# ScalarE's one-hots spread over two tiles, an earlier gate load, and doubled row slots moved to other tiles

## The reference, cut to what matters

```
g   = softmax(best_s)                                  # 8 heads x 16 experts
act = gelu(einsum('thkd,td->thk', u_tab[expert], x)) * g
out = einsum('thk,thkd->td', act, v_tab[expert])
```

## Time and profile before

| | us |
|---|---|
| three runs, median | 2750.67 |
| lowest and highest | 2739.39, 2750.81 |
| the profiled execution | 2743.88 |
| its span, first to last instruction | 2742.1 |
| tiles 26 to 89 of scoring | 1221.82 to 1678.12 |
| tiles 106 to 121 | 1797.25 to 1898.80 |
| the seam: last two tiles of scoring to the first of combining | 1920.66 to 1955.10 |
| combining | 1955.10 to 2718 |

### The profile page before, as it was taken

The page is one execution under the profiler, slowest core; times in us unless marked ns, Lnnn a source line. Parts: engine busy times, 40 slices in busy tenths (PEclk is TensorE's granted clock), DMA queues, the critical chain, the costliest instruction groups (busy, mean ns, idle before and its releaser), DMA issues.

```text
span 2742.1 us, 34124 instructions
## 1 busy us (share of the span) xinstructions
PE 2401.4 (88%) x10438; PEld 1873.8 (68%) x10438; DVE 2054.3 (75%) x3817; ACT 1140.9 (42%) x2430; POOL 982.4 (36%) x665
## 2 busy tenths in 40 slices
PE   4987888999899787888888889999688999999996
PEld 3767766666456566666776767778567777777775
DVE  4867713666388855888887888866678888888888
ACT  2332043444311143236666667786233333333333
POOL 2013104422032321684675856686212222222220
PEclk9999999999999899999999999999899999999998
DMA  7646654333032325577989989899899999999996
GB/s 275 218 162 253 255 218 154 123 123 113 25 119 101 146 77 188 129 180 263 313 248 311 283 274 298 272 301 357 319 377 368 369 388 388 392 390 389 393 389 237
DMA packets 276170, 697.78 MB, mean 254 GB/s; under 512 B 52832, under 2 KB 164832, under 8 KB 234848
## 3 DMA queue, kind: packets, MB, share of 16 engines
q1 hardware_dynamic: 182624, 384.03, 39.8%
q0 software_dynamic: 74496, 270.70, 28.5%
q10 hardware_dynamic: 18944, 41.95, 4.2%
HBM read 614.67 MB, written 81.92 MB: 254 GB/s over the span
## 4 chain that ended last, share of the span: by engine, by line
PE 48%; DVE 21%; ACT 8%; DMA 7%; DVEq 5%; issue 5%; ACTq 4%; SPq 1%; POOL 0%; PEldq 0%; PEld 0%
PE ps L897 26%; PE ps L588 7%; PE ps L573 4%; DVE arena L1492 3%; ACTq L1350 3%; DMA act_in<-act_scratch 2%; DVEq L1856 2%; PE ps L937 2%; PE ps L600 2%; DVE g_acc L1844 2%; DVE rows L1835 2%; DVE t_lo L1915 2%; DMA arena<-in_weights 2%; ACT hot L1302 1%; DMA ring<-in_weights 1%
## 5 line engine op out<-in xcount | busy, mean ns | idle before, releaser
L1282 ACT CAST t_hi<-raw 128x1024 fp32r<-128x1024 f32 x256 | 268.6, 1049 | 726.5 <-PE ps L897 707.8
L2045 POOL DMA_INDIRECT rows<-in_rows,pick_e x256 | 289.2, 1129 | 779.7 <-DVE g_acc L1844 719.3
L2056 POOL DMA_INDIRECT gate_scratch<-cell_g,cell x256 | 454.1, 1774 | 157.5 <-DVE cell_g L1830 81.6
L897 PE MATMUL ps<-t_hi,c_hi 128*128 128x512 f32 x1024 | 408.5, 399 | 65.5 <-DVE t_lo L1915 45.9
L897 PE MATMUL ps<-n_hi,t_hi 128*128 128x512 f32 x1024 | 413.1, 403 | 31.9 <-DVE t_lo L1861 23.1
L1980 POOL TENSOR_TENSOR w_lo<-ring,w_hi 128x1024 fp32r<-128x1024 f32 x76 | 190.5, 2512 | 666.4 <-ACT w_hi L1035 559.1
L897 PE MATMUL ps<-n_lo,t_hi 128*128 128x512 f32 x1024 | 404.2, 395 | 0.0
L897 PE MATMUL ps<-n_hi,t_lo 128*128 128x512 f32 x1024 | 403.6, 394 | 0.0
L897 PE MATMUL ps<-t_hi,c_lo 128*128 128x512 f32 x1024 | 400.9, 391 | 0.0
L897 PE MATMUL ps<-t_lo,c_hi 128*128 128x512 f32 x1024 | 400.8, 391 | 0.0
L1844 DVE SCALAR_TENSOR_TENSOR g_acc<-rows,small,g_acc 128x1024 f32<-128x1024 f32 x254 | 326.4, 1285 | 94.0 <-ACT small L1351 78.2
(11 more groups left out here) (207 smaller groups left out, 3939.5 us busy)
## 6 DMA issues: line engine op xcount, KB each, us to landing
raw<-in_table SPq DMA_DIRECT2D x256, 512.0 KB, 8.5
ring<-in_weights SPq DMA_DIRECT2D x44, 2048.0 KB, 8.2
act_scratch<-act_out SPq DMA_DIRECT2D x128, 256.0 KB, 4.3
act_in<-act_scratch SPq DMA_DIRECT2D x128, 256.0 KB, 10.7
gate_in<-gate_scratch SPq DMA_DIRECT2D x32, 1024.0 KB, 13.8
arena<-in_weights ACTq DMA_DIRECT2D x24, 1024.0 KB, 9.4
gate_scratch<-score_in SPq DMA_DIRECT2D x16, 1024.0 KB, 11.9
gate_scratch<-staged ACTq DMA_DIRECT2D x8, 2048.0 KB, 9.6
```

The lines of the kernel that those rows point to most:

```text
L897: last = mm(out, a, b_, start=start and x == 0, stop=stop and x == len(pairs) - 1, skip_group_check=True)
L1282: copy(t_hi[:, t % 2, :], raw[:, t % 4, :]).then_inc(hi_ready, 1)
L2045: G.indirect_dma_start(rows[:, j % 4, :], None, rows_in, bass.IndirectOffsetOnAxis(ap=pick_e[:, j:j + 1], axis=0)).then_inc(row_in[j % 4], 16)
L2056: G.indirect_dma_start(gate_cells, bass.IndirectOffsetOnAxis(ap=cell[:, n:n + 1], axis=0), cell_g[:, n:n + 1], None, compute_op=ALU.add).t ...
```

## The change

`scale_hot` is cut in two. The Abs part becomes `spread_hot`; for steps 1 to 31 it is issued at the end of the tile before the step's own, and for step 0 and steps 32 to 63 where it was. The Relu part stays. The wait for the step two before moves with the Abs. `slots_of` gives the tiles 124 to 127 one slot each, the even tiles 106 to 120 two, and in combining every eighth tile two (16 of them) where it was every sixth (20). On SP the first gate load, with the waits ahead of it, moves from behind the last two stores of activations to behind the raw load of tile 131, one tile earlier in the program. The buffers of `t_hi` and `t_lo` stay at two.

```diff
--- before.py
+++ after.py
@@ -317,14 +317,12 @@
 
             if k < DENSE:
                 return ()
-            if k < P - 4:
-                return (k - DENSE,)
             if k < P:
-                j = P - 4 - DENSE + 2 * (k - P + 4)
-                return (j, j + 1)
+                j = k - DENSE + min(max(k - 105, 0) // 2, 8)
+                return (j, j + 1) if k % 2 == 0 and 106 <= k <= 120 else (j,)
             v = k - P
-            j = P - DENSE + 4 + v + min((v + 2) // 6, 20)
-            return (j, j + 1) if v % 6 == 3 and v < 120 else (j,)
+            j = P - DENSE + 8 + v + (v + 4) // 8
+            return (j, j + 1) if v % 8 == 3 else (j,)
 
         def starts(s):
             return 2 * s if s < DENSE // 2 else DENSE + 4 * (s - DENSE // 2)
@@ -499,16 +497,17 @@
                 for x in range(2, 2 * len(PAIRS)):
                     if starts(x - 1) == k:
                         load_scores(sp, False, x)
+                if k == P - 1:
+                    for half in range(2):
+                        sp.wait_ge(gates_stored[half], 16 * STEPS // 16)
+                        sp.wait_ge(scattered[half], 16 * TOPK * HEADS)
+                    load_gates(0, 0)
                 if k == P // 2:
                     for t in range(4):
                         load_act(0, t)
                 if k:
                     store_act(k - 1)
             store_act(P - 1)
-            for half in range(2):
-                sp.wait_ge(gates_stored[half], 16 * STEPS // 16)
-                sp.wait_ge(scattered[half], 16 * TOPK * HEADS)
-            load_gates(0, 0)
 
             def step(i, t, half, last=False):
 
@@ -1292,7 +1291,7 @@
                 act.wait_ge(tile_done, k + (P - 1))
                 copy(c_hi[:, t % 2, :], act_in[:, t % 4, :]).then_inc(c_hi_ready, 1)
 
-            def scale_hot(s):
+            def spread_hot(s):
 
                 col = 4 * (s % 32)
                 after(act, g_done, s - 1)
@@ -1300,6 +1299,10 @@
                     if s < 32:
                         A(hot1[:, s % 2, x, :], iota, ACT.Abs, bias=sel_n[:, 0, col + x:col + x + 1])
                     A(hot2[:, s % 2, x, :], iota, ACT.Abs, bias=sel_n[:, 1, col + x:col + x + 1])
+
+            def scale_hot(s):
+
+                col = 4 * (s % 32)
                 act.drain()
                 if s < 32:
                     A(hot1[:, s % 2], hot1[:, s % 2], ACT.Relu, bias=ones[:, 0:1], scale=-1.0)
@@ -1368,9 +1371,14 @@
                 if k - 1 in TURN_AT:
                     take_block(1 + TURN_AT.index(k - 1))
                 for s in steps_of(k):
+                    if s % 32 == 0 or s > 32:
+                        spread_hot(s)
                     scale_hot(s)
                     if s:
                         copy_gates(s - 1)
+                for s in steps_of(k + 1):
+                    if 0 < s < 32:
+                        spread_hot(s)
                 if k == P - 6:
                     copy_gates(STEPS - 1)
                 for j in slots_of(k)[1:]:
```

## The result

The changed kernel takes 2727.99 us, the median of ten runs (2720.88 to 2733.64), against 2750.74 for the kernel before in ten runs beside them: a ratio of 0.993, 95% interval 0.9914 to 0.9947. It is faster, by 22.8 us, about half of what I forecast.

A forecast was written before the change was run, and what follows sets the result against it. TensorE was busy 88% of the span, so time could come only from its waits, which differ by stage. Terms -31 + 9 - 15.5 - 7 = -44.5 took 2743.9 to 2699.4, forecast as 2700 us, 80% range 2678 to 2730.

The forecast's parts named there:

- Spreading: Score tiles, steps 1 to 31: moving the Abs a tile ahead removes waits for hot2g; -31 us, between -50.5 and -20.
- POOL's lag: Score tiles while a pair's scatters are sent: POOL falls behind 5.8 us a pair, 2 lost four times, 8 us.
- the 16 tiles over 108 us: Sign against the prediction: 16 score tiles, 112.8 us before and forecast near 103, staying over 108.
- The 39 us for VectorE alone: Score tiles: VectorE's 48.7 us of idle time less 9.6 that stays, the spreading gain before POOL's lag.
- Doubled slots: Tiles 106 to 120: eight added gathers on a full POOL cost +9 us, between 0 and +15.
- today's lead: Tiles 106 to 120: 4 us of the gathers' existing lead, counted once, taken off the cost of doubled slots.
- longer instructions: Tiles 106 to 120: 2 us added to the cost of doubled slots for longer scatters.
- bound of +15: Tiles 106 to 120: upper end of the forecast cost of the doubled slots, in us.
- POOL paces the trains and the doubled tiles: Rival for score tiles: POOL sets the pace, spreading gives only -20, doubled slots cost +15; 2716 us, chance 0.17.
- the rival that I held at 4 in 100: Scatters in the trains and doubled tiles stretch beside denser VectorE row work, making the kernel slower; 2771 us, chance 0.04.
- Seam: Between scoring and combining: gate load issued at 1923.6 instead of 1939.11, PE idle about 8 us; -15.5 us, -10 to -21.
- Combining: Combining half: 16 doubled tiles for 20 save 6.3 us, plus 0.7 at the first output block; -7 us, -5 to -9.

The follow-up runs named there:

- e7: Changed kernel with two scatters a tile from 24 to 95, no doubled tiles in scoring, all 24 in combining at every fifth tile; 2702.9 us, ratio 0.9853.
- e8: Changed kernel with two scatters a tile from 24 to the end of scoring, three in every eighth tile from 96; 2710.81 us, ratio 0.9878.
- e10: e7 with its 24 doubled combining tiles at every fourth tile instead of every fifth; 2711.86 us, ratio 0.9845.
- e9: Changed kernel with the sixteen doubled tiles of combining moved two tiles away from the gate load; 2730.5 us, ratio 0.9934.
- e1: Kernel before with only the Abs of steps 1 to 31 moved a tile ahead, old slots and gate load; 2731.1 us, ratio 0.9943.
- e3: Kernel before with only the first gate load moved ahead of the last two stores; 2741.1 us, ratio 0.9978.
- e4: Changed kernel with the slots of the kernel before, so spreading and early gate load only; 2721.6 us, ratio 0.9919.
- e5: The even pace: changed kernel with two scatters a tile from 24 to 95 in place of three and two; 2715.75 us, ratio 0.9884.

## Why the prediction was half right

*Spreading* (forecast -31, measured -19.5). The step itself was right: the Abs hide in the odd tile, and while rows are in time hot2g is too, in all but the tile of a pair's Exp. The step that failed is POOL's lag, 8 us. I had POOL's need for four tiles right, 27.1 us (27.2 measured, with shorter scatters and longer gathers than I took), but set it against 25.3 us for the tiles, a mean over 16 with the slow tile of the pair in it. While the scatters are sent, four tiles take 23.6 us, so POOL falls behind by 3.6 us and not by 1.8: 11.5 us in a pair's 12.8 tiles, not 5.8. The even pace gives 456.3 - 424.2 = 32 us (35.5 in e7, e8 and e10), and the bunched scatters take 12.6 to 16 of these where I had 8. I had said that the 16 tiles over 108 us would make the prediction wrong: they took 110.4.

The 39 us for VectorE alone were too many as well. That 16 tiles with an even pace take 103.4 us, where I had put them near 103, is partly luck: PE, which idles in only 3 of them, sets the pace in the rest, and the tile of a pair's Exp, of whose 4.4 us I let 2.5 go, kept 4.6.

*Doubled slots* (forecast +9, bound +15, measured +22.8): the largest miss. The eight gathers at 10.7 were not too few: six of them fall in the stretch. The two other parts were wrong. I took off 4 us for today's lead. It gave nothing lasting: POOL was full, and the row loop added 9.1 us of waiting instead. And I put 2 us for longer instructions, where 10.7 were lost. The bound of +15 held no room for either; a cost over 20 us was the second thing that I had named as proof of an error. My rival "POOL paces the trains and the doubled tiles" (2716) named the mechanism, at too low a price.

In the changed kernel 29 of the 38 scatters of that stretch overlap a row dot or row add and take 1.99 us on the mean, the nine others 1.60; before it was 25 at 1.82 and 14 at 1.57 (counted over the timelines of POOL and VectorE). So more of them met VectorE's row work, and those that did were longer. That is the mechanism of the rival that I held at 4 in 100, in one of its two places; in tiles 34 to 49 the scatters did not stretch (1.74 us for 1.83), only the gathers did (1.38 for 1.10). The overlap is a correlation in the traces; no run took VectorE's row work away from the scatters. The rule of the Trainium skill, "SBUF — State Buffer", Who interferes with whom, is that a VectorE instruction with two SBUF inputs contends with a GpSimd one that reads SBUF, and that their shared port pair is an exclusive lock; the trace agrees in direction, with 0.4 us for an overlapped scatter on the mean, against 1.2 to 1.3 us for a row instruction.

*Seam* (forecast -15.5; tile 126 to the first of combining went from 34.44 to 18.41). Right by its own steps: load 2.5 us after my 1923.6, as tile 126 itself began 2.2 us later, landing near the median, idle 7.37 for about 8. By the parts run alone, single last tiles give 11 us of it and the early load 4. The landing decides: 12.9 us here, 17.9 in e9.

*Combining* (forecast -7, measured -1.3 from tile 128 to the end). The step that failed is that I counted no row wait at all for the new places: 15.7 us of them stand in combining. e9, with the doubled tiles moved and no row wait, takes 779.1 us from tile 128 to the end, for 785.7. The -1.3 itself is one profile's: from tile 128 to 254 the five kernels with the new places take 753.1 to 755.9 us and the four with the old ones (before, e1, e3, e4) 757.1 to 760.4.

The errors: 11.5 + 13.8 + 5.7 + 1.4 at the seam (its last two tiles and the four ahead of them) = 32.4, less 3.1 in the stretches that I had at nothing: 29.3. Forecast and profile differ by 44.5 - 15.2 = 29.3. That the medians differ by 22.8 and not by 15.2 is the spread of single executions (before's profiled one was 6.8 us under its median) and isn't mine to claim.

## What to carry to other kernels

An in-order queue that is full in a stage has no cheap extra work: price the added instructions, the longer ones around them, and the loop in which a late result delays the next request. When a wait is removed, look next at the queue that feeds the engine that now sets the pace; how the work in it is spread can be worth as much as the wait (e5: 12.6 us for one line). Set a queue's need against the pace of the very tiles beside it, not against a mean over the stage. Where doubled transfers stand among large ones is worth a run of its own.

## What the runs showed of the hardware that I had not expected

The first 1 MB gate load took 19.3 and 19.7 us from issue to first use in the two kernels with two row gathers in each of those tiles and the load moved forward, and 12.1 to 17.9 in those with one; with the same code up to there and nearly the same issue time it took 12.9 in the changed kernel's profile and 17.9 in e9's. So a seam read from one execution is known to some 5 us. Ahead of the gate step of tile 121 PE of the changed kernel waits 3.16 us; tile 122 then takes 7.5 us at a granted clock of 0.72, part of it at the lower level, 1.2 GHz, and the next tile 5.4 us at 1.00. In e9 PE waits 2.87 us at the same step, and tile 122 takes 5.6 us at 1.00. So one such wait cost 2 us more than itself and a like one nothing.
